# Two S5 half-units of the up-projection moved into the delta scan, and its first loads issued at the scan's start

## The chip, the cores and the metric

One core of a Trainium2 chip runs the whole kernel in one launch. The metric is the device time of that launch in microseconds (us), the median of the runs. TensorE (PE; its weight loads are PEld) multiplies into PSUM, which has 8 banks here (`P[:, 0..7, :]`); VectorE (DVE) and ScalarE (ACT) read PSUM; GpSimd (POOL) works on SBUF; SyncE (SP) issues most of the DMAs, in the order of its program, and waits on semaphores between them.

## The reference, cut to what matters

One step of a decoder block on 1024 prompt tokens and 8 x 4 sample tokens (NT = 1056 in all), D = 1024. A projection gives q, k, v, z, gates and the S5 input. Two branches run: a gated delta rule over chunks of 64 tokens, with 8 heads of 64, and an S5 branch. They are merged, and a mixture of experts follows:

```python
o = _rmsnorm(o, head_norm_w) * jax.nn.silu(z)          # o: output of the delta scan
y_a = o.reshape(bsz, t, DN_WIDTH) @ w_a_up             # 512 -> 1024
ys = ys * jax.nn.sigmoid(ys @ w_glu)                   # S5 branch
y_b = ys @ w_b_up                                      # 512 -> 1024
mixed = (sigmoid(gate_a) * y_a + sigmoid(gate_b) * y_b) @ w_o
x = x + mixed
x = x + _hier_moe(_rmsnorm(x, norm_ffn_w), ...)
```

All of it is float32. y_b needs only the S5 branch, which is done (and stored in DRAM as `y2_d`) before the scan begins.

## The kernel before, in words

The order of the work on each engine is written out by hand; engines meet through semaphores only. A large SBUF tile (`arena`) holds everything at hand-chosen offsets, so a load can only begin when what lay at its offset has been read.

**Delta scan** (L1041 to L1080 on PE, 16 chunks c = 0..15). PE in chunk c: state product (L1047, needs the state `s_S >= c+1`), query product (L1056), then for chunk c+1 the two products that need no state (`w_chunk` L1025, `u_chunk` L1036), then a wait for `s_kb` (POOL's scaled keys, L631) and `s_vn` (DVE's copy of the chunk's new values, L1739), then the state update product (L1066) and the output product (L1071). DVE in chunk c: copy `vn` (L1739), scale the state (L1740), add the update (L1742, sets `s_S`), then in the early chunks a step of the sample tokens' recurrence (L1695 to L1712), and in chunks 11 and 12 (`SQ_AT + 4`, `SQ_AT + 5`) two `head_norm`s each (L1730, L1732) for the first third of the tokens. PE's head sums for that third (L1079) are in chunks 8 and 9 and use banks 4 and 5; `s_rf` counts ACT's reads of them. Banks 0 and 1 take L1036/L1047, 2 and 3 the outputs, 6 and 7 the rest.

**Up-projection** (L1093 to L1107 on PE). The tokens are cut into three thirds of TBK = 352, the output features into KD = 8 blocks of 128: 24 units u, third u // 8, block u % 8. A unit is two halves of four matmuls (k = 0..3) of 128x128 by 128x352: the delta half `WAU` x `QT` and the S5 half `WBU` x `Y2`; a float32 matmul has two records in the trace. Units use the banks (0,1), (2,3), (4,5) in turn. After each of the first 8 units PE does a head sum (L1090) for the later thirds. DVE multiplies each half with its gate and adds (L1767 to L1769), and counts `s_yf`. Before u = 0 PE waits for `s_o2 >= 4` (head norms of the first third) and `s_wbu >= 32` (WBU and the first third of Y2 loaded); before every unit from 3 on for the read of the banks' last content.

**SP's queue** around it: at the scan's start (`s_S >= 1`) two loads of z (L2682) and the gate loads of units 0 to 3 (L2679); then, in chunks 9 to 12, the stores and the load for the sample tokens (L2693 to L2697); after `s_kb >= 48` (POOL has done its last chunk) the load of WBU (L2701, 2048 KB) and the three thirds of Y2 (L2703, 704 KB each), each third issued when the one before has landed; then the final state's store, the further gate loads (each behind `s_yf`) and W_O (L2717). Once the up-projection is done (`s_mix`), PE goes on with L1147 and SP with the loads of the next stage (L2720 and after).

Of the kernel before, what the change touches and what calls it, by code (L numbers as in the profile page):

```python
# [16 lines left out]
D = 1024  # L17
# [4 lines left out]
KD = D // 128  # L22
TT_ = (NT + 127) // 128
H, DH = 8, 64
HP = H // 2
C = 64
NC_ = SEQ // C
# [21 lines left out]
NBK = 3  # L49
TBK = NT // NBK  # L50
TSTRIP = NT // 4
KB0 = TBK // L
ARENA = 50020
# [18 lines left out]
def hybrid_step(nc, x_p, x_s, st_conv, st_delta, st_re, st_im, norm_mix, w_in, conv_w, a_log, dt_bias, head_norm,  # L72
# [4 lines left out]
    with ctx:  # L77
# [12 lines left out]
        y2_d = dram("y2_d", (SW // 128, 128, NT))  # L90
# [30 lines left out]
        def at(off, *dims):  # L121
            n = 1
            for d in dims:
                n *= d
            v = arena[:, off:off + n]
            if len(dims) == 2:
                return v.rearrange("p (a b) -> p a b", a=dims[0])
            if len(dims) == 3:
                return v.rearrange("p (a b c) -> p a b c", a=dims[0], b=dims[1])
            return v  # L130
# [5 lines left out]
        STG = WR + NWR * KD * 128  # L136
        stage = [at(STG + i * L * KS, L * KS) for i in range(2)]
        R = STG + 2 * L * KS
# [73 lines left out]
        QT = at(r, HP, NT)  # L212
# [5 lines left out]
        PRo = r + 4096  # L218
# [18 lines left out]
        WAU = at(WR, 4, D)  # L237
        MIX = at(R, KD, NT)
        PAIR = SEQ - 128
        PAIRED = NT - PAIR  # L240
        q = R + 8448 + HP * NT
        WBU = at(q, 4, D)
        x1 = at(q, TT_, D)
        GT = [at((5632, q + 9216)[j] + i * 2 * TBK, 2, TBK) for j in range(2) for i in range(4)]
        ZT = [at(q + 15360 + i * HP * TBK, HP, TBK) for i in range(2)]
        SQ2 = [at(o, HP, TBK) for o in (R + 4912, q + 18432, q + 18432 + HP * TBK)]
        OSN = at(ARENA - 1124, HP, 128)
        Y2 = at(q + 4096, 4, NT)
        SQ_AT = 7

        NWE = 3
# [72 lines left out]
        P = ctx.enter_context(nc.psum_tensor("P", [128, 8, 512], F32))  # L324
# [55 lines left out]
        s_selo = sem("s_selo")  # L380
# [13 lines left out]
        s_ou = sem("s_ou")  # L394
# [6 lines left out]
        s_rf = sem("s_rf")  # L401
# [4 lines left out]
        s_wbu = sem("s_wbu")  # L406
        s_gt = [sem("s_gt0"), sem("s_gt1")]
        s_ya = sem("s_ya")
        s_yf = sem("s_yf")
# [47 lines left out]
        s_inv = sem("s_inv")  # L457
# [240 lines left out]
        def _(pe):  # L698
# [51 lines left out]
            for i in range(TT_):  # L750
                n = rows(i)
                b = 6 - 2 * (i % 2)
                pe.wait_ge(s_xs, i + 1)
                pe.wait_ge(s_6f, max(i, 1))
                for k in range(KD):
                    m = pe.matmul(P[:, b + k // 4, 128 * (k % 4):128 * (k % 4) + n], xt[i][0:n, 128 * k:128 * k + 128],  # L756
                                  scale_of[i % 2][0:n, 0:n], start=True, stop=True)
# [59 lines left out]
            for a in range(GA):  # L817
                o = bank[:, 2 * GC * a:2 * GC * (a + 1)]
                pe.matmul(o, tmp[0][:, 128 * a:128 * a + 128], CTp[0][:, a].rearrange("p b c -> p (b c)"),
                          start=True, stop=False)  # L820
                m = pe.matmul(o, tmp[1][:, 128 * a:128 * a + 128], CTp[1][:, a].rearrange("p b c -> p (b c)"),
                              start=False, stop=True)
# [62 lines left out]
            for j in range(4):  # L885
                for q, (s0, sn) in enumerate(((0, 3), (3, 3), (6, 2))):
# [4 lines left out]
                    for k in range(4):  # L891
                        m = pe.matmul(bank[:, 0:sn * KS], wglu[:, k, 128 * j:128 * j + 128],  # L892
                                      ygT[:, k, s0:s0 + sn, :].rearrange("p a b -> p (a b)"),
                                      start=k == 0, stop=k == 3)
# [125 lines left out]
            def w_chunk(c):  # L1020
                pe.wait_ge(s_kb, 3 * c + 1)
                bank = bank7()
                for hp in range(HP):
                    for h in heads:
                        i = pe.matmul(bank[h, 64 * hp:64 * hp + 64], KB[c % 2][h, hp, :], TB[hp][h, c, :], start=True,  # L1025
                                      stop=True)
                i.then_inc(s_7, 1)

            def u_chunk(c):

                pe.wait_ge(s_kb, 3 * c + 2)
                if c >= 2:
                    pe.wait_ge(s_vn, c - 1)
                for hp in range(HP):
                    for h in heads:
                        pe.matmul(P[h, c % 2, 64 * hp:64 * hp + 64], TB[hp][h, c, :], VB[c % 2][h, hp, :],  # L1036
                                  start=hp == 0, stop=False, skip_group_check=True)

            w_chunk(0)
            u_chunk(0)  # L1040
            for c in range(NC_):  # L1041
                pe.wait_ge(s_wT, c + 1)
                pe.wait_ge(s_S, c + 1)
                S = S2[c % 2]
                for hp in range(HP):
                    for h in heads:
                        i = pe.matmul(P[h, c % 2, 64 * hp:64 * hp + 64], wT[c % 2][h, hp, :], S[h, hp, :],  # L1047
                                      start=False, stop=hp == HP - 1, skip_group_check=True)
                i.then_inc(s_vu, 1)

                if c >= 2:
                    pe.wait_ge(s_oc, c - 1)
                ob = P[:, 2 + c % 2, :]
                for hp in range(HP):
                    for h in heads:
                        pe.matmul(ob[h, 64 * hp:64 * hp + 64], S[h, hp, :], QT[h, hp, 64 * c:64 * c + 64], start=hp == 0,  # L1056
                                  stop=False, skip_group_check=True)
                if c + 1 < NC_:
                    w_chunk(c + 1)
                    u_chunk(c + 1)  # L1060
                pe.wait_ge(s_kb, 3 * c + 3)
                pe.wait_ge(s_vn, c + 1)
                bank = bank6()
                for hp in range(HP):
                    for h in heads:
                        i = pe.matmul(bank[h, 64 * hp:64 * hp + 64], KDr[c % 2][h, hp, :], vn[c % 2][h, hp, :],  # L1066
                                      start=True, stop=True)
                i.then_inc(s_6, 1)
                for hp in range(HP):
                    for h in heads:  # L1070
                        i = pe.matmul(ob[h, 64 * hp:64 * hp + 64], vn[c % 2][h, hp, :], KQ[h, hp, c, :], start=False,  # L1071
                                      stop=hp == HP - 1, skip_group_check=True)
                i.then_inc(s_ou, 1)
                if c in (SQ_AT + 1, SQ_AT + 2):
                    for hp in range(2 * (c - SQ_AT - 1), 2 * (c - SQ_AT)):
                        pe.wait_ge(s_sq2, hp + 1)
                        if hp >= 2:
                            pe.wait_ge(s_rf, hp - 1)
                        pe.matmul(P[:, 4 + hp % 2, 0:TBK], head_ones[:], SQ2[0][:, hp, :], start=True,  # L1079
                                  stop=True).then_inc(s_sm, 1)  # L1080
# [12 lines left out]
            for u in range(NBK * KD):  # L1093
                m, t = u % KD, TBK * (u // KD)
                if m == 0:
                    pe.wait_ge(s_o2, HP * (u // KD + 1))
                    pe.wait_ge(s_wbu, 16 * (2 + u // KD))
                if u >= 3:
                    pe.wait_ge(s_yf, u - 2)
                b = 2 * (u % 3)  # L1100
                for o, w, v in ((b, WAU, QT), (b + 1, WBU, Y2)):
                    for k in range(4):
                        i = pe.matmul(P[:, o, 0:TBK], w[:, k, 128 * m:128 * m + 128], v[:, k, t:t + TBK], start=k == 0,  # L1103
                                      stop=k == 3)
                i.then_inc(s_ya, 1)
                if u < 2 * HP:
                    head_sum(HP + u)  # L1107
# [218 lines left out]
        def _(dve):  # L1326
# [278 lines left out]
            for n in QSTEPS:  # L1605
                m = n - 1
# [150 lines left out]
            dve.sem_inc(s_os, 1)  # L1757
            dve.wait_ge(s_so, 1 + 64)
            for u in range(NBK * KD):
                b = 2 * (u % 3)  # L1760
                m, t = u % KD, TBK * (u // KD)
                dve.wait_ge(s_tb[u % 4], 32 + 16 * (u // 4 + 1))
                gt = GT[u if u < 4 else 4 + u % 4]
                ga, gb = gt[:, 0, :], gt[:, 1, :]
                ya, yb, o = P[:, b, 0:TBK], P[:, b + 1, 0:TBK], MIX[:, m, t:t + TBK]
                dve.wait_ge(s_ya, u + 1)
                link(dve.tensor_tensor(o, ya, ga, ALU.mult))  # L1767
                link(dve.tensor_tensor(gb, yb, gb, ALU.mult))
                dve.tensor_tensor(o, o, gb, ALU.add).then_inc(s_yf, 1)  # L1769
                dve.wait_ge(s_yf, u + 1)  # L1770
                if u in (4, 5, 9, 10):
                    j = {4: HP, 5: HP + 2, 9: 2 * HP, 10: 2 * HP + 2}[u]
                    head_norm(j)
                    head_norm(j + 1)
# [759 lines left out]
        def _(sp):  # L2534
# [140 lines left out]
            def gates(u):  # L2675
                m, t = u % KD, TBK * (u // KD)
                if u >= 4:
                    sp.wait_ge(s_yf, u - 3)
                sp.dma_start(GT[u if u < 4 else 4 + u % 4], gate_d[:, m, :, t:t + TBK].rearrange("j p t -> p j t")).then_inc(s_tb[u % 4], 16)  # L2679
# [4 lines left out]
            sp.wait_ge(s_S, 1)  # L2684
            gate_of_heads(0)
            gate_of_heads(1)
            for u in range(4):
                gates(u)

            sp.wait_ge(s_so, 1)  # L2690
            for v in range(2):
# [6 lines left out]
            sp.wait_ge(s_o2, HP)  # L2698
            gate_of_heads(2)
            sp.wait_ge(s_kb, 3 * NC_)  # L2700
            sp.dma_start(WBU, w_b_up[0].rearrange("(k p) n -> p k n", p=128)).then_inc(s_wbu, 16)  # L2701
            for t in range(NBK):
                sp.dma_start(Y2[:, :, TBK * t:TBK * t + TBK],  # L2703
                             y2_d[:, :, TBK * t:TBK * t + TBK].rearrange("k p t -> p k t")).then_inc(s_wbu, 16)
                sp.wait_ge(s_wbu, 16 * (2 + t))

            sp.wait_ge(s_S, NC_ + 1)
            for b in range(2):
# [105 lines left out]
```

## Time and profile before

| | us |
|---|---|
| median of 3 runs (lowest, highest) | 1516.19 (1514.94, 1517.57) |
| the profiled execution's own time | 1514.86 |
| its span, first to last instruction | 1513.1 |
| PE busy in the span | 1386.5 (92%) |
| DVE busy | 743.9 |
| DMA queue of SP and ACT (q1), share of 16 engines | 39.9% |

PE's idle time is spread in small pieces. The scan runs from about 770 to 845 us, the up-projection from 849.5 to 971 us. The granted clock (PEclk) is a share of full speed: 1.00 is 2.4 GHz and 0.50 is 1.2 GHz. In the names of transfers the numbers of buffers are left out, so `y_d` stands for `y2_d` at L2703. Busy spans of PE overlap a little (a matmul's end is modelled), so starts are the safer figures.

### The profile page before, as it was taken

How to read it: one execution, taken by the hardware profiler on the slowest of the kernel's cores; microseconds unless marked ns; L12 is line 12 of the kernel's file. 1: busy time of each engine (PE TensorE's matmuls, PEld its weight loads, DVE VectorE, ACT ScalarE, POOL GpSimd, SP SyncE). 2: the span in 40 equal slices, each digit the busy share in tenths (PEclk: the TensorE clock that was granted, in tenths of full speed). 3: DMA queues.
4: the chain of work that ended last, by engine and by line, in shares of the span. 5: the costliest groups of instructions: out<-in, count | busy, mean ns of one | idle time of the engine just before them, and what ended most of it. 6: DMA issues, size and time to landing. Idle time of an engine off the chain costs nothing.

```text
span 1513.1 us, 26998 instructions
## 1 busy us (share of the span) xinstructions
PE 1386.5 (92%) x11499; PEld 967.5 (64%) x11499; DVE 743.9 (49%) x1376; ACT 389.9 (26%) x707; POOL 147.5 (10%) x152
## 2 busy tenths in 40 slices
PE   7999999999999999999967899999978999999906
PEld 6667666666666656656767666765547888888802
DVE  4667695403425532689687344355553433222324
ACT  4211100114536553232213110011112333333312
POOL 1000010000001000045036000001111000000031
PEclk9998999999999999999989899999979999999958
DMA  5243684543522113233331425334348999999755
GB/s 170 82 102 57 188 239 134 134 122 103 140 62 62 44 44 99 53 99 119 92 136 32 157 69 187 108 131 155 112 154 326 420 425 426 426 425 425 304 183 195
DMA packets 190050, 262.54 MB, mean 174 GB/s; under 512 B 61219, under 2 KB 159889, under 8 KB 181465
## 3 DMA queue, kind: packets, MB, share of 16 engines
q1 hardware_dynamic: 164668, 200.39, 39.9%
q10 hardware_dynamic: 16988, 30.29, 5.4%
q0 software_dynamic: 8256, 29.89, 5.3%
q8 instruction: 103, 1.69, 0.5%
q14 instruction: 35, 0.28, 0.1%
HBM read 184.64 MB, written 75.90 MB: 172 GB/s over the span
## 4 chain that ended last, share of the span: by engine, by line
PE 75%; DVE 9%; DMA 5%; issue 5%; ACT 3%; POOL 2%; ACTq 0%; POOLq 0%; SPq 0%; DVEq 0%
PE P L730 28%; PE P L1103 8%; PE P L1292 6%; PE P L1190 5%; PE P L1261 4%; PE P L1289 3%; DMA arena<-in_w_expert_up_dram 2%; PE P L892 2%; POOL arena L631 2%; PE P L1226 1%; PE P L1265 1%; PE P L756 1%; PE P L1147 1%; DVE arena L1601 1%; PE P L954 1%
## 5 line engine op out<-in xcount | busy, mean ns | idle before, releaser
L730 PE MATMUL P<-arena 128*128 128x352 f32 x1680 | 520.8, 465 | 4.0 <-ACT arena L2363 2.8
L730 PEld LDWEIGHTS P<-arena 128*128 128x128 f32 x1680 | 315.9, 191 | 184.5 <-issue 23.4
L1289 PE MATMUL P<-arena 128*32 128x384 f32 x1536 | 172.8, 490 | 2.3 <-DMA arena<-in_w_expert_up_dram 2.3
L1292 PE MATMUL P<-arena 128*32 128x128 f32 x1536 | 174.9, 274 | 0.0
L1292 PEld LDWEIGHTS P<-arena 128*32 128x32 f32 x1536 | 165.8, 110 | 0.3
L1103 PE MATMUL P<-arena 128*128 128x352 f32 x384 | 117.9, 468 | 3.8 <-DMA arena<-y_d 3.8
L1103 PEld LDWEIGHTS P<-arena 128*128 128x128 f32 x384 | 74.4, 194 | 45.6 <-issue 6.1
L1261 PE MATMUL P<-arena 128*32 128x512 f32 (+1 forms) x768 | 89.5, 488 | 1.5 <-DVE arena L2013 1.5
L1265 PE MATMUL P<-arena 128*32 128x256 f32 x384 | 88.7, 380 | 0.0
L1190 PE MATMUL P<-arena 128*128 128x512 f32 x192 | 87.0, 598 | 0.0
L1965 DVE COPY arena<-P 128x512 f32<-128x512 f32 x24 | 16.6, 691 | 111.2 <-PE P L1226 109.9
L1289 PEld LDWEIGHTS P<-arena 128*32 128x32 f32 x1536 | 60.6, 110 | 6.5 <-DMA arena<-in_w_expert_up_dram 3.0
L2504 ACT ACTIVATE arena<-P 32x128 f32<-32x128 f32 x96 | 26.0, 270 | 141.9 <-PE P L1292 141.1
L2488 ACT ACTIVATE arena<-P 32x768 f32<-32x768 f32 (+2 forms) x56 | 45.0, 804 | 64.1 <-PE P L1265 63.9
L1976 DVE COPY arena<-P 32x256 f32<-32x256 f32 x96 | 40.4, 421 | 42.7 <-PE P L1265 41.6
L1190 PEld LDWEIGHTS P<-arena 128*128 128x128 f32 x192 | 34.9, 190 | 36.0 <-issue 35.9
L2091 ACT ACTIVATE arena<-P 128x1056 f32<-128x1056 f32 x20 | 21.0, 1050 | 134.9 <-PE P L730 134.2
L1620 DVE SCALAR_TENSOR_TENSOR arena<-arena,par 128x1024 f32<-128x1024 f32 x36 | 46.3, 1285 | 13.6 <-ACT arena L2296 12.7
L631 POOL TENSOR_TENSOR arena<-arena,N 128x256 f32<-128x256 f32 x48 | 44.7, 931 | 76.3 <-ACT arena L2387 26.0
L1767 DVE TENSOR_TENSOR arena<-P,arena 128x352 f32<-128x352 f32 x24 | 12.6, 525 | 77.7 <-PE P L1103 77.7
L1261 PEld LDWEIGHTS P<-arena 128*32 128x32 f32 x768 | 34.9, 109 | 19.4 <-issue 3.7
L1265 PEld LDWEIGHTS P<-arena 128*32 128x32 f32 x384 | 40.3, 110 | 10.5
(420 smaller groups left out, 1854.1 us busy)
## 6 DMA issues: line engine op xcount, KB each, us to landing
arena<-in_w_expert_up_dram SPq DMA_DIRECT2D x32, 2048.0 KB, 16.6
arena<-in_w_expert_down_dram SPq DMA_DIRECT2D x32, 1024.0 KB, 11.1
arena<-in_w_in_dram SPq DMA_DIRECT2D x36, 512.0 KB, 4.2
x_d<-zero SPq DMA_DIRECT2D x4, 3072.0 KB, 21.4
arena<-x_d POOLq DMA_DIRECT2D x24, 512.0 KB, 10.7
y_d<-arena ACTq DMA_DIRECT2D x24, 512.0 KB, 9.7
y_d<-zero SPq DMA_DIRECT2D x8, 1152.0 KB, 7.8
gate_d<-arena ACTq DMA_DIRECT2D x16, 528.0 KB, 4.3
```

The costliest lines, as they stand in the source:

```text
L631: pool.tensor_tensor(ring[c % 2], src[:, :, c, :], N1[:, q, :, c].unsqueeze(2).broadcast_to([128, HP, C]), ALU.mult).then_inc(s_kb, 1)
L730: m = pe.matmul(P[:, b + j, 0:TBK], w[:, k, :], hT[:, k, TBK * j:TBK * j + TBK], start=f, stop=l)
L892: m = pe.matmul(bank[:, 0:sn * KS], wglu[:, k, 128 * j:128 * j + 128], ygT[:, k, s0:s0 + sn, :].rearrange("p a b -> p (a b)"), start=k == ...
L1103: i = pe.matmul(P[:, o, 0:TBK], w[:, k, 128 * m:128 * m + 128], v[:, k, t:t + TBK], start=k == 0, stop=k == 3)
L1190: m = pe.matmul(P[:, b + o, :], MIX[:, k, 128 * i:128 * i + 128], W_O[:, k, 512 * o:512 * o + 512], start=k == 0, stop=k == KD - 1)
L1261: m = pe.matmul(P[strip_of(slot_of(i, s)[1]), b + o, 0:n], rows_of[s][:, k, :], WD[i % NWE][:, k, 512 * o:512 * o + n], start=k == 0, stop ...
L1265: m = pe.matmul(P[strip_of(slot_of(i, NSTRIP)[1]), b + o, FF * j:FF * j + FF], rows_of[s][:, k, :], WD[i % NWE][:, k, D - FF:D], start=k = ...
L1289: m = pe.matmul(P[strip_of(s), i % 2, 0:384], rows_of[s], WU[i % NWE][:, k, 128:512], start=k == 0, stop=k == KD - 1, skip_group_check=True)
L1292: m = pe.matmul(P[RT:128, i % 2, 128 * s:128 * s + 128], rows_of[s], WU[i % NWE][:, k, 0:128], start=k == 0 and s == 0, stop=k == KD - 1, ...
L1620: link(dve.scalar_tensor_tensor(acc[:, 0:SEQ], raw[:, i:i + SEQ], wcol, acc[:, 0:SEQ], ALU.mult, ALU.add))
L1976: m = dve.tensor_copy(yo[c % 3][strip_of(slot_), D - FF:D], P[last, 2 + 2 * (i % 2) + s // 2, FF * (s % 2):FF * (s % 2) + FF])
L2488: m = act.activation(yo[c % 3][h, 0:D - FF], wide[h, 0:D - FF], ACT.Copy)
```

## The change

The first three gate buffers, half of WBU at a time and the first third of Y2 get offsets that are free from the scan's start. SP loads them there; the S5 halves of units 0 and 1 are multiplied in chunks 11 and 12. `second_half` stands in PE's chunk after `u_chunk` and ahead of the waits for `s_kb` and `s_vn`. Unit 3's gate load and the second copy of WBU's upper half go to the end of the scan.

```diff
-        GT = [at((5632, q + 9216)[j] + i * 2 * TBK, 2, TBK) for j in range(2) for i in range(4)]
+        GT = [at(o, 2, TBK) for o in (R + 6400, R + 6400 + 2 * TBK, STG + 1024, q + 21248)]
+        GT += [at(q + 9216 + i * 2 * TBK, 2, TBK) for i in range(4)]
+        WBU_EARLY = [at(PRo, 2, D), at(5632, 2, D)]
+        Y2_EARLY = [at(o, TBK) for o in (7680, 7680 + TBK, STG + 1024 + 2 * TBK, ARENA - 612)]
+        def unit_banks(u):
+            return ((0, 5), (1, 4), (2, 3))[u] if u < 3 else (2 * (u % 3), 2 * (u % 3) + 1)
+        UNITS_READ = [0, 0, 0, 2, 3, 3]
+        def wbu(k, u):
+            return WBU[:, k, :] if k >= 2 and u >= KD else WBU_EARLY[k // 2][:, k % 2, :]
+        def y2(k, u):
+            return Y2_EARLY[k] if u < KD else Y2[:, k, TBK * (u // KD):TBK * (u // KD) + TBK]
...
+            def second_half(u):
+                for k in range(4):
+                    i = pe.matmul(P[:, unit_banks(u)[1], 0:TBK], wbu(k, u)[:, 128 * (u % KD):128 * (u % KD) + 128], y2(k, u),
+                                  start=k == 0, stop=k == 3)
+                return i
...
                     w_chunk(c + 1)
                     u_chunk(c + 1)
+                if c in (SQ_AT + 4, SQ_AT + 5):
+                    pe.wait_ge(s_wbu, 16 * 6)
+                    pe.wait_ge(s_rf, HP)
+                    second_half(c - SQ_AT - 4)
                 pe.wait_ge(s_kb, 3 * c + 3)
                 pe.wait_ge(s_vn, c + 1)
...
-                    pe.wait_ge(s_wbu, 16 * (2 + u // KD))
+                    pe.wait_ge(s_wbu, 16 * (6, 8, 9)[u // KD])
                 if u >= 3:
-                    pe.wait_ge(s_yf, u - 2)
-                (both halves of every unit)
+                    pe.wait_ge(s_yf, UNITS_READ[u] if u < len(UNITS_READ) else u - 2)
+                (the delta half; then)
+                if u >= 2:
+                    i = second_half(u)
...
             gate_of_heads(1)
-            for u in range(4):
+            sp.wait_ge(s_inv, 1)
+            sp.wait_ge(s_selo, HP)
+            for u in range(3):
                 gates(u)
+            for j in range(2):
+                sp.dma_start(WBU_EARLY[j], wb_view[:, 2 * j:2 * j + 2, :]).then_inc(s_wbu, 16)
+            for k in range(4):
+                sp.dma_start(Y2_EARLY[k], y2_d[k][:, 0:TBK]).then_inc(s_wbu, 16)
...
             sp.wait_ge(s_kb, 3 * NC_)
-            sp.dma_start(WBU, ...).then_inc(s_wbu, 16)
-            for t in range(NBK):
+            sp.dma_start(WBU[:, 2:4, :], wb_view[:, 2:4, :]).then_inc(s_wbu, 16)
+            for t in range(1, NBK):
                 sp.dma_start(Y2[:, :, TBK * t:TBK * t + TBK], ...).then_inc(s_wbu, 16)
-                sp.wait_ge(s_wbu, 16 * (2 + t))
+                sp.wait_ge(s_wbu, 16 * (7 + t))
+            sp.wait_ge(s_ou, NC_)
+            gates(3)
```

## Rows read from the trace of the kernel before

**Rows 1.** The page: busy us of each engine (share) xinstructions; shares of the chain that ended last.
```profile
PE 1386.5 (92%) x11499; PEld 967.5 (64%) x11499; DVE 743.9 (49%) x1376; ACT 389.9 (26%) x707; POOL 147.5 (10%) x152
PE 75%; DVE 9%; DMA 5%; issue 5%; ACT 3%; POOL 2%; ACTq 0%; POOLq 0%; SPq 0%; DVEq 0%
```
**Rows 2.** Chain of waits, 818 to 971 us: start, us, what.
```profile
818.36 1.38 PE P L1079 x4
...
838.89 10.49 DMA arena<-y_d
...
849.52 7.78 PE P L1103 x16
857.29 0.59 PE P L1090 x2
857.89 4.73 PE P L1103 x16
...
895.16 75.75 PE P L1103 x256
```
**Rows 3.** Timeline, chunks 11 and 12: start, us, engine, line [idle before <-releaser].
```profile
824.29 0.68 PE L1047 MATMUL P<-arena 64*64 64x64 f32 x16 [0.21 <-DVE arena L1742]
...
825.01 0.42 DVE L1739 COPY arena<-P 128x256 f32<-128x256 f32 x1 [0.87 <-PE P L1047]
...
826.12 0.58 PEld L1066 LDWEIGHTS P<-arena 64*64 64x64 f32 x16
...
827.52 0.68 PE L1047 MATMUL P<-arena 64*64 64x64 f32 x16 [0.21 <-DVE arena L1742]
...
828.88 0.58 PEld L1036 LDWEIGHTS P<-arena 64*64 64x64 f32 x16
...
830.77 0.42 DVE L1739 COPY arena<-P 128x256 f32<-128x256 f32 x1
...
831.26 0.68 PEld L1066 LDWEIGHTS P<-arena 64*64 64x64 f32 x16 [1.80 <-issue]
...
832.73 0.57 PEld L1047 LDWEIGHTS P<-arena 64*64 64x64 f32 x16 [0.33 <-issue]
```
**Rows 4.** Timeline, PE's last group before the up-projection.
```profile
845.32 0.40 PE L1085 MATMUL P<-shift_id,arena 32*128 32x32 f32 x4 [0.26 <-DVEq L1745]
```
**Rows 5.** Timeline, state products of chunks 1, 2, 3.
```profile
774.81 0.68 PE L1047 MATMUL P<-arena 64*64 64x64 f32 x16 [0.21 <-DVE arena L1742]
...
779.43 0.68 PE L1047 MATMUL P<-arena 64*64 64x64 f32 x16 [0.21 <-DVE arena L1742]
...
784.05 0.68 PE L1047 MATMUL P<-arena 64*64 64x64 f32 x16 [0.21 <-DVE arena L1742]
```
**Rows 6.** Windows of 2 us: busy by engine, then PEclk, DMA share, GB/s.
```profile
774.00:776.00 2.00, 1.79 (x62) 1.68 (x59) 1.61 (x2) 0.38 (x1) 1.18 (x2) 1.00 1.06 394
...
782.00:784.00 2.00, 1.15 (x32) 1.04 (x32) 1.31 (x4) 0.14 (x2) 1.33 (x3) 1.00 0.03 8
...
838.00:840.00 2.00, 2.00 (x43) 2.00 (x44) 0.76 (x2) 0.11 (x1) 0.45 (x1) 0.53 1.16 356
...
852.00:854.00 2.00, 2.00 (x5) 1.25 (x4) 0.00 (x0) 0.00 (x0) 0.00 (x0) 0.50 0.53 196
```
**Rows 7.** Timeline, state products of chunks 14 and 15, and the gap before 14.
```profile
836.54 0.68 PE L1066 MATMUL P<-arena 64*64 64x64 f32 x16 [1.69 <-issue]
...
837.89 0.97 PE L1047 MATMUL P<-arena 64*64 64x64 f32 x16 [0.21 <-DVE arena L1742]
...
842.67 0.68 PE L1047 MATMUL P<-arena 64*64 64x64 f32 x16 [0.21 <-DVE arena L1742]
```
**Rows 8.** Landing times of L2703 (Y2, x3), L2679 (gates, x24).
```profile
DMA to landing us min/median/max: 4.1/4.4/10.5
DMA to landing us min/median/max: 2.9/3.2/11.3
```
**Rows 9.** Timeline, the first of DVE's three operations on unit 0.
```profile
857.44 0.52 DVE L1767 TENSOR_TENSOR arena<-P,arena 128x352 f32<-128x352 f32 x1 [11.29 <-PE P L1103]
```

More of the change, by code:

```diff
@@ L1096, in _ @@
                     pe.wait_ge(s_o2, HP * (u // KD + 1))
-                    pe.wait_ge(s_wbu, 16 * (2 + u // KD))
+                    pe.wait_ge(s_wbu, 16 * (6, 8, 9)[u // KD])
                 if u >= 3:
-                    pe.wait_ge(s_yf, u - 2)
[L1100 to L1104, printed above, removed]
+                    pe.wait_ge(s_yf, UNITS_READ[u] if u < len(UNITS_READ) else u - 2)
+                for k in range(4):
+                    i = pe.matmul(P[:, unit_banks(u)[0], 0:TBK], WAU[:, k, 128 * m:128 * m + 128], QT[:, k, t:t + TBK], start=k == 0, stop=k == 3)
+                if u >= 2:
+                    i = second_half(u)
                 i.then_inc(s_ya, 1)
@@ L1759, in _ @@
             for u in range(NBK * KD):
-                b = 2 * (u % 3)
                 m, t = u % KD, TBK * (u // KD)
@@ L1764, in _ @@
                 ga, gb = gt[:, 0, :], gt[:, 1, :]
-                ya, yb, o = P[:, b, 0:TBK], P[:, b + 1, 0:TBK], MIX[:, m, t:t + TBK]
+                ya, yb, o = *[P[:, b, 0:TBK] for b in unit_banks(u)], MIX[:, m, t:t + TBK]
                 dve.wait_ge(s_ya, u + 1)
@@ L2686, in _ @@
             gate_of_heads(1)
-            for u in range(4):
+            sp.wait_ge(s_inv, 1)
+            sp.wait_ge(s_selo, HP)
+            for u in range(3):
                 gates(u)
+            wb_view = w_b_up[0].rearrange("(k p) n -> p k n", p=128)
+            for j in range(2):
+                sp.dma_start(WBU_EARLY[j], wb_view[:, 2 * j:2 * j + 2, :]).then_inc(s_wbu, 16)
+            for k in range(4):
+                sp.dma_start(Y2_EARLY[k], y2_d[k][:, 0:TBK]).then_inc(s_wbu, 16)
             sp.wait_ge(s_so, 1)
@@ L2700, in _ @@
             sp.wait_ge(s_kb, 3 * NC_)
-            sp.dma_start(WBU, w_b_up[0].rearrange("(k p) n -> p k n", p=128)).then_inc(s_wbu, 16)
-            for t in range(NBK):
+            sp.dma_start(WBU[:, 2:4, :], wb_view[:, 2:4, :]).then_inc(s_wbu, 16)
+            for t in range(1, NBK):
                 sp.dma_start(Y2[:, :, TBK * t:TBK * t + TBK],
                              y2_d[:, :, TBK * t:TBK * t + TBK].rearrange("k p t -> p k t")).then_inc(s_wbu, 16)
-                sp.wait_ge(s_wbu, 16 * (2 + t))
+                sp.wait_ge(s_wbu, 16 * (7 + t))
+            sp.wait_ge(s_ou, NC_)
+            gates(3)
             sp.wait_ge(s_S, NC_ + 1)
```

## The prediction

> **What bounds the kernel now.** The page first: PE is busy for 92% of the span, and 75% of the chain that ended last is PE [rows 1]. So a change pays only if PE's own work or PE's waits become less in the stage it touches, and everything behind it starts from PE. The chain of waits, read next over the stage, shows where PE is not the bound: at 838.89 it lies in the first Y2 load (queued behind WBU's, and issued when POOL had done its last chunk), stays there 10.49 us, and comes back to PE at 849.52 with unit 0 of the up-projection [rows 2]. The timeline says what PE did meanwhile: it finished the scan with the sample transposes at 845.32 + 0.40 = 845.72 and then stood still until 849.52, 3.8 us [rows 2, 4]. The same chain shows a second loss: unit 0 takes 7.78 us and every later unit 4.73 [rows 2]. The windows give the cause: the granted clock is 0.50 in 852 to 854 (1.2 GHz), after the standstill [rows 6]. From 895.16 on there is nothing but PE, 16 records per unit, without a wait, until 895.16 + 75.75 = 970.91 [rows 2]. The scan itself is bound by a ring PE, DVE, POOL whose gaps differ from chunk to chunk, so the question is which gap the moved work meets.
>
> **The change, part by part.** One matmul is two records of 4.73 / 16 = 0.296 us [rows 2], so the half of a unit is 8 records, 2.37 us.
>
> (a) Two S5 halves leave the up-projection: 2 x 2.37 = 4.73 us off PE, in a stage where PE is the bound. Nothing else is there to be late: DVE needs three operations of about 0.52 us per unit, 1.6 us, and even the shortened units 0 and 1 last 2.37 us and a head sum of 0.59 [rows 2, 9].
>
> (b) The standstill of 3.8 us [rows 2, 4] goes, since at the scan's end unit 0 waits for nothing that is still on its way. What is late next? Unit 0 needs only WAU, the head norms of the first third and early loads. The first head sum (L1090) needs ACT's squares of the next third, which in the trace follow the scan's end at once; unit 0's 2.37 us cover one of them. I take the whole 3.8; the least it can be is 3.5, if the start costs a wait as short as the 0.2 to 0.3 seen elsewhere [rows 3, 4].
>
> (c) Unit 0 ran at half clock after the standstill: 7.78 - 4.73 = 3.05 us [rows 2]. Without the standstill PE passes from the scan to dense matmuls at once, and I take all of it. Bounds: 0, if the clock is low there for another reason, and 3.05.
>
> (d) Chunk 11. `second_half(0)` stands in PE's order ahead of the state update. DVE's head norms of chunk 11 come after that update, so they cannot hide it. In the trace PE goes from L1036 straight to L1066 at 826.12 while its input, `vn`, has been there since 825.01 + 0.42 = 825.43 [rows 3]: no gap at all. So this half lies wholly on the path. Its price: four records of a head sum inserted in the same way took 1.38 us in the chain [rows 2], 0.20 more than 4 x 0.296; for 8 records 2.37 + 0.20 = 2.57 us. Queued behind it are the update, the output product and the next chunk of all three engines; they all move by 2.57. Bounds: 0, if something unseen covers it, and 4.7 + 0.2 = 4.9 at half clock.
>
> (e) Chunk 12. Now DVE's two head norms of chunk 11 (from about 827.52) delay `vn` of chunk 12 to 830.77, and PE, whose last weights of L1036 began at 828.88, could go on 0.47 us later (its step between such groups), at 829.35, but goes on at 831.26 [rows 3]: a gap of 1.91. It hides 1.91 of the 2.57; 0.66 us is left on the path. Bounds: 0 and 4.9 - 1.9 = 3.0. Chunk 13 has the like gap, behind the second pair of head norms (1.69 us [rows 7]), and gets nothing.
>
> (f) The early loads. Three gates of 352 KB, 2048 KB of WBU, 704 KB of Y2 and the two loads of z of 704 KB make 5.2 MB (before: four gates and the z, 2.8 MB); at 394 GB/s [rows 6] that is an estimated 13 to 14 us from about 771, landed by 785 to 790. PE wants them at 826: `s_wbu >= 96` and `s_rf >= 4` (ACT read the last head sum at about 820) cost nothing. Do they slow the chunks beside them? Chunk 1 to 2 with the DMA engines full took 779.43 - 774.81 = 4.62 us, chunk 2 to 3 with almost no DMA after 780 took 784.05 - 779.43 = 4.62 [rows 5, 6]. Nothing, so nothing is charged; the nearest bound on the other side is a few tenths.
>
> (g) The loads at the scan's end are shorter (half of WBU, two thirds of Y2), but unit 3's gates now stand behind both Y2 waits and `s_ou`. With the scan 3.2 us later, SP begins at about 841.7; WBU's half and Y2 no later than the 10.5 us of before, 852.2; the next Y2 4.4 (median) and the gates 3.2 [rows 8]: landed at about 860. DVE wants them with unit 3's product. Starting at 848.9, units 0 and 1 take 2.96 each, unit 2 5.32, unit 3's product is there at 864.9. Covered, by 5 us. Further gates, W_O, the second third's Y2 and upper half of WBU (needed at unit 8) have tens of us.
>
> (h) Chunk 14 ran at half clock: granted 0.53 in 838 to 840, and from state product to state product 842.67 - 837.89 = 4.78 us where chunk 11, with the same work at full clock, took 827.52 - 824.29 = 3.23 [rows 3, 6, 7]: 1.5 us lost. The gap of 1.69 us before it [rows 7] stays, so I let this loss stay too: 0, with bounds of -1.5 (it goes) and +1.5 (a second chunk falls as this one did).
>
> Sum: -4.73 - 3.8 - 3.05 + 2.57 + 0.66 = -8.35 us. The end of the up-projection moves from 971 to about 962.5. Behind it SP's loads for the next stage and PE's L1147 both start from its end, so the shift is passed on whole. Against the profiled execution's own time: 1514.86 - 8.4 = 1506.5. That execution was at the low end of the runs (1514.94 to 1517.57, median 1516.19); taken off the median, 1507.8, which I forecast.
>
> A rule that bears on (h): the Trainium skill, "TensorE: Matmul & The Clock Gate", Part 1, ties the fall of the clock to an idle engine and its return to activity. Read strictly, with the inserted work in chunks 11 and 12 the engine would be kept awake.
>
> **The rivals.**
>
> *The low stretch before chunk 14 goes too.* The two halves add 4.7 us of PE work within 10 us ahead of it. For it: more work of PE just ahead of the place. Against: the gap right before the fall is not filled [rows 7]. It would give 1.5 us more: 1507.8 - 1.5 = 1506.3. (This is the outcome that the page just named would have; the trace speaks half for it, since the clock fell with gaps of under 2 us, where the page thinks of an engine that stands idle.)
>
> *The half clock at the start of the up-projection stays.* A fall shortly before the scan's end would reach into unit 0. For it: chunk 14 fell, and a low stretch like it that begins one chunk later would lie partly in unit 0. Against: the low clock of unit 0 followed a standstill that is gone [rows 2, 6]. It costs up to 3.05: 1507.8 + 3.05 = 1510.8.
>
> *The gain is not passed on.* The path behind has stages with other limits (DMA in the chain is 5%, [rows 1]); if scatter and clock in them take back 4 to 8 us, the time is about 1514. Nothing in the rows speaks for it but that PE's clock is not the same in every execution.
>
> *Slower: unit 3's gates come too late.* Its place is DVE before unit 3; PE runs on until unit 6, which needs unit 3 read: 864.9 + 0.6 + 2 x 5.32 = 876.1. So the landing decides from 876.1 - 1.6 = 874.5 on, each us later costs one, and beyond 874.5 + 8.4 = 882.9 the kernel is slower than before; at 885 it would be 1516.2 + 2.1 = 1518.3. For it: three transfers in a row, each behind a wait, on one queue. Against: even with the longest landing of each row, 841.7 + 10.5 + 10.5 + 11.3 = 874.0 [rows 8].
>
> **How the numbers follow.** Forecast 1507.8: 0.62. Low stretch gone, 1506.3: 0.14. Half clock stays, 1510.8: 0.14. Not passed on, 1514: 0.08. Gates late, 1518.3: 0.02. The lower end: the forecast with -1.5 of (h), 0.66 of (e) hidden and about 1.3 of scatter (the runs' half width), 1504.4. The upper end: (c) lost and another chunk at half clock, 1507.8 + 3.05 + 1.5 = 1512.3. A change of under 0.2% (3.0 us) cannot be told from none; faster than 1513.2: the first three and a quarter of the fourth, 0.92; same: 0.05; slower, 0.03, of which 0.02 is the late gates and 0.01 things unseen.
>
> **What would show it.** (a) Units 0 and 1 with 8 records each. (b) The first matmul of unit 0 within 0.3 us of L1085. (c) Unit 2, the first whole one, at 4.73, and PEclk 1.00 from there. (d) L1066 of chunk 11 some 2.5 us later behind `vn` than before, and the state products of 11 and 12 5.8 us apart, not 3.23. (e) Those of 12 and 13 about 5.9 apart; before, 832.76 - 827.52 = 5.24 (832.73 is the start of chunk 13's weights) [rows 3]. (f) The chunks before 11 as before. (g) No idle of DVE before unit 3 on a DMA. Wrong would be: a wait on a DMA in chunk 11, a scan longer by more than 4 us, a low clock in the first units, or an up-projection that ends near 962 with a kernel that is not 8 us shorter.

## The result, and the profile after

| | before | changed |
|---|---|---|
| median as first measured (runs) | 1512.45 (6) | 1501.89 (6) |
| ratio, 95% interval | | 0.9927 [0.9898, 0.9956] |
| mean of the runs beside all kernels of this study | 1513.0 (98) | 1502.2 (19) |
| span of the profiled execution | 1513.1 | 1495.1 |

(The 18 further runs that repeat the kernel before, in the experiments, have a mean of 1513.3.)

The kernel became faster by 10.8 us (means), 0.7%, and the ratio's interval leaves out 1. Forecast were 8.4 us less and 1507.8 us, with a range from 1504.4: the time lies below the range. The forecast difference alone, 8.4 of 1512.45 us or a ratio of 0.9944, lies inside the interval; the parts below show what it was made of.

The page of the changed kernel, busy us and shares of the chain (before: [rows 1]):

```profile
PE 1379.1 (92%) x11499; PEld 963.3 (64%) x11499; DVE 742.3 (50%) x1376; ACT 390.2 (26%) x707; POOL 147.8 (10%) x152
PE 76%; DVE 8%; DMA 6%; issue 4%; ACT 3%; POOL 2%; ACTq 0%; POOLq 0%; SPq 0%; DVEq 0%
```

Its lines have moved: L1058 is `second_half`, L1070 the state product (L1047 before), L1093 the state update (L1066), L1128 the delta half of a unit (L1103), L1117 the head sum (L1090), L1173 the next stage (L1147), L1343 PE's first matmul of the last part (L1317). The chain of waits over the stage, start, us, what (before: [rows 2]):

```profile
822.49 2.56 PE P L1058 x8
825.05 0.64 PE P L1093 x16
...
828.44 2.56 PE P L1058 x8
831.00 0.61 PE P L1093 x16
...
844.80 0.40 PE P L1112 x4
845.20 2.56 PE P L1128 x8
847.77 0.59 PE P L1117 x2
848.36 2.37 PE P L1128 x8
...
853.68 2.37 PE P L1058 x8
...
960.89 17.65 PE P L1173 x128
```

The 10.49 us in a DMA are gone from the chain; PE passes from the transposes (844.80) to unit 0 (845.20) without a gap; unit 0's half takes 2.56 us and not twice that; units 0 and 1 have one half each. The window 846 to 852 says the same of the clock (its last columns: PEclk, DMA share, GB/s; before, 0.50 in [rows 6]):

```profile
846.00:852.00 6.00, 6.00 (x21) 3.82 (x21) 2.63 (x6) 3.36 (x8) 0.00 (x0) 1.00 0.46 135
```

The price, in the timeline of chunks 11 and 12 (before: [rows 3]):

```profile
820.41 0.68 PE L1070 MATMUL P<-arena 64*64 64x64 f32 x16 [0.21 <-DVE arena L1768]
...
821.13 0.42 DVE L1765 COPY arena<-P 128x256 f32<-128x256 f32 x1 [0.87 <-PE P L1070]
...
822.42 2.63 PE L1058 MATMUL P<-arena 128*128 128x352 f32 x8
...
826.36 0.68 PE L1070 MATMUL P<-arena 64*64 64x64 f32 x16 [0.23 <-DVE arena L1768]
...
829.60 0.42 DVE L1765 COPY arena<-P 128x256 f32<-128x256 f32 x1
...
832.30 0.68 PE L1070 MATMUL P<-arena 64*64 64x64 f32 x16 [0.22 <-DVE arena L1768]
```

In chunk 11 the copied values were there at 821.55 and PE worked on the half until about 824.98: 5.95 us from state product to state product, before 3.23. In chunk 12, 832.30 - 826.36 = 5.94, before 5.24.

Cut into three, the kernel shows what moved. "Stage" runs from the scan's first state product to the first matmul of the next stage; "middle" from there to the end of the last expert tile; "last part" from there to the last instruction. "Scan" is the part of the stage up to the end of PE's sample transposes:

| kernel (profiles) | scan | stage | middle | last part |
|---|---|---|---|---|
| before (3) | 75.5, 73.1, 73.8 | 202.6, 200.1, 201.4 | 468.9, 470.7, 468.0 | 71.5, 71.9, 73.0 |
| changed (3) | 78.6, 80.1, 79.6 | 194.3, 195.8, 195.3 | 468.1, 466.3, 471.1 | 66.1, 68.7, 66.9 |

In means the stage gives 6.3 us, the last part 4.9, and the middle is the same within its scatter of some 5 us. The last part is the surprise: nothing of the change is in it.

### The profile page after: what moved, and what is told of

The parts are those of the page before. It is cut to its first block, busy times and chain, and to the rows that moved or that the text cites. A ratio compares the mean times of both kernels' runs of the same rounds, so it can differ in the third digit from the quotient of the medians.

```text
span 1495.1 us, 27006 instructions
## 1 busy us (share of the span) xinstructions
PE 1379.1 (92%) x11499; PEld 963.3 (64%) x11499; DVE 742.3 (50%) x1376; ACT 390.2 (26%) x707; POOL 147.8 (10%) x152
## 4 chain that ended last, share of the span: by engine, by line
PE 76%; DVE 8%; DMA 6%; issue 4%; ACT 3%; POOL 2%; ACTq 0%; POOLq 0%; SPq 0%; DVEq 0%
PE P L747 28%; PE P L1318 6%; PE P L1216 5%; PE P L1058 4%; PE P L1128 4%; DMA arena<-in_w_expert_up_dram 4%; PE P L1287 3%; PE P L1315 3%; PE P L909 2%; PE P L1252 1%; PE P L1291 1%; PE P L1173 1%; DVE arena L1627 1%; PE P L879 1%; PE P L940 1%
## 5 line engine op out<-in xcount | busy, mean ns | idle before, releaser
L1318 PEld LDWEIGHTS P<-arena 128*32 128x32 f32 x1536 | 166.9, 111 | 0.6
L1315 PEld LDWEIGHTS P<-arena 128*32 128x32 f32 x1536 | 61.0, 111 | 6.5 <-DMA arena<-in_w_expert_up_dram 3.0
L1058 PE MATMUL P<-arena 128*128 128x352 f32 x192 | 60.9, 460 | 0.0
L1128 PE MATMUL P<-arena 128*128 128x352 f32 x192 | 60.8, 460 | 0.0
L1128 PEld LDWEIGHTS P<-arena 128*128 128x128 f32 x192 | 36.4, 190 | 20.1
L1058 PEld LDWEIGHTS P<-arena 128*128 128x128 f32 x192 | 36.3, 190 | 20.0
L1287 PEld LDWEIGHTS P<-arena 128*32 128x32 f32 x768 | 34.9, 109 | 19.4 <-issue 3.7
## 6 DMA issues: line engine op xcount, KB each, us to landing
arena<-x_d POOLq DMA_DIRECT2D x24, 512.0 KB, 10.8
```

Source lines behind the costliest of these rows:

```text
L1058: i = pe.matmul(P[:, unit_banks(u)[1], 0:TBK], wbu(k, u)[:, 128 * (u % KD):128 * (u % KD) + 128], y2(k, u), start=k == 0, stop=k == 3)
L1128: i = pe.matmul(P[:, unit_banks(u)[0], 0:TBK], WAU[:, k, 128 * m:128 * m + 128], QT[:, k, t:t + TBK], start=k == 0, stop=k == 3)
L1287: m = pe.matmul(P[strip_of(slot_of(i, s)[1]), b + o, 0:n], rows_of[s][:, k, :], WD[i % NWE][:, k, 512 * o:512 * o + n], start=k == 0, stop ...
L1315: m = pe.matmul(P[strip_of(s), i % 2, 0:384], rows_of[s], WU[i % NWE][:, k, 128:512], start=k == 0, stop=k == KD - 1, skip_group_check=True)
L1318: m = pe.matmul(P[RT:128, i % 2, 128 * s:128 * s + 128], rows_of[s], WU[i % NWE][:, k, 0:128], start=k == 0 and s == 0, stop=k == KD - 1, ...
```

## Experiments

**Both kernels again, unaltered.** For second and third profiles (the first of each is in the table above).

> The changed kernel once more, unaltered, timed beside the kernel before. Theory A (stage sum): it is 8.4 us shorter than before, in four parts that a second profile repeats: scan 3.2 us longer (770.2 to 845.7 us before: 75.5 us; here 78.7), standstill gone, unit 0 at full clock, two halves less; everything outside scan and up-projection differs only by what differs between two executions of one kernel. Theory B: the change also shortens what lies behind the up-projection (in the first profile 540.3 us before, 534.2 after), by another 5 to 6 us, and a second profile and the times show that again: 13 to 15 us shorter than before.

> The kernel before once more, unaltered, for a second profile. Theory A: scan 75.5 us with chunk 11 at 3.23 us, standstill 3.8 us, unit 0 at 7.8 us again; what lies before the scan and behind the up-projection differs from the first profile by several us (the changed kernel's profiles: 534.2 and 535.0 us behind it, two experiments 539.0 and 543.8), which shows that this part is scatter and not the change. Theory B: behind the up-projection it takes 540 us again, within 1 us.

> The kernel before, third profile. Behind the up-projection its first two took 540.3 and 542.5 us, five kernels with the changed scan 533.9 to 543.8. If that part is scatter alone, this one may lie anywhere in 534 to 544; if the change shortens it by 4 to 6 us (theory B), it lies at 540 or above again. From the scan's first state product to the next stage: 200.1 to 202.6 us again.

> The changed kernel, third profile. Scan's first state product to next stage 194.3 to 195.7 us again, or 1.5 less if chunk 14 runs at full clock (then 192.8 to 194.2). Behind it 534.2 and 535.0 us so far: scatter alone allows 534 to 544, theory B wants below 536. Time 8 to 9 us below before.

Measured: the changed kernel 1503.14 (ratio 0.9941 [0.9919, 0.9963]) and 1502.15 (0.9923 [0.9906, 0.9941]); the kernel before against itself 1.001 [0.9991, 1.0029] and 1.0 [0.9987, 1.0012]. Chunk 11 is 3.23, 3.23, 3.23 before and 5.95, 5.95, 5.95 after. What lies behind the up-projection as a whole (middle and last part) is 540.3, 542.5, 541.0 us before and 534.2, 535.0, 538.0 after: the two sets don't overlap, but 538.0 is above the 536 that theory B wanted, and theory B says nothing of where. The whole times decide nothing either: the medians are 9.3 and 11.8 us below before, where theory A wanted 8.4 and theory B 13 to 15. Nor did the scan repeat as expected. Chunk 14 ran at full clock in the second and third profile of before and in the third of the changed kernel, and there the stage was 195.3 us, not the expected 192.8 to 194.2. The time was lost in chunk 15, which took 4.47 us and not 3.06. Its state product stops after 14 of its 16 records, at full clock and with no wait in the profile:

```profile
847.32 0.27 PE L1070 MATMUL P<-arena 64*64 64x64 f32 x1 [1.12 <-issue]
```

In the second profile of before, the chain of waits at the scan's end:

```profile
836.35 10.07 DMA arena<-y_d
846.42 0.14 issue
846.55 6.65 PE P L1103 x16
```

The standstill is 4.9 us there and not 3.8, since the scan ended at 841.63 (chunk 14 at full clock: 3.22 us, not 4.78) while the load, begun at POOL's last chunk, landed no sooner after it; and unit 0 took 6.65 us, not 7.78. So the standstill and unit 0's slow start trade against each other. From the scan's end to the next stage the kernel before takes 127.1, 127.1 and 127.6 us in its three profiles (standstills of 3.8, 4.9 and 5.0 us, unit 0 at 7.78, 6.65 and 7.12 us), and the changed kernel 115.7 in all three.

**Loads only: the halves go back to units 0 and 1.**

```diff
-                if c in (SQ_AT + 4, SQ_AT + 5):
-                    ...
-                    second_half(c - SQ_AT - 4)
-                if u >= 2:
-                    i = second_half(u)
+                i = second_half(u)
```

> The early loads stay, the two S5 halves go back from chunks 11 and 12 into units 0 and 1. Theory A: scan as long as before (75.5 us), up-projection without standstill and at full clock, 4.7 us longer than in the changed kernel; in all 6.9 us shorter than before, and 4.73 - 3.23 = 1.5 us longer than the changed kernel. Rival: halves put in chunks are hidden, so this is 4.7 us longer than the changed kernel.

Measured: 1507.25 us, 0.9965 [0.9949, 0.9981]. Chunk 11 is 3.23 us again, and from the scan's end to the next stage it takes 120.4 us against 115.7 in the changed kernel: 4.7 more, two halves. Against the 2.7 + 0.7 us that the halves cost in chunks 11 and 12, moving them is worth 1.3 us. Stage 194.1 us, with chunk 14 at full clock (1.5 us of luck). The early loads alone bring most of the stage's gain. The whole is 5.3 us below before by the ratio, expected were 6.9. The whole time is 4 us above the changed kernel, as the rival wanted, but its last part is 71.2 us (below), so it is no proof of the rival.

The early loads have a price that this kernel shows by itself, since it has them without the halves. In chunk 3, after 351 matmul records counted from the scan's first, PE stops inside a group with no wait in the profile:

```profile
784.37 0.27 PE L1053 MATMUL P<-arena 64*64 64x64 f32 x1 [1.31 <-issue]
```

All fifteen profiles of kernels with the early loads have this pause at this very record (0.76 to 1.59 us), and none of the five without them (before, and before with redundant waits, below). Chunk 3 takes 4.8 us in place of 4.4, in means; chunks 0 to 10 together take 54.3 in place of 53.4.

**Halves in chunks 12 and 13.**

```diff
-                if c in (SQ_AT + 4, SQ_AT + 5):
+                if c in (SQ_AT + 5, SQ_AT + 6):
                     ...
-                    second_half(c - SQ_AT - 4)
+                    second_half(c - SQ_AT - 5)
```

> The two halves in chunks 12 and 13, behind the head norms, in place of 11 and 12. Theory A: chunk 11 is 3.23 us again from state product to state product; each half meets a gap of 1.91 and 1.69 us and leaves 0.7 and 0.9 us on the path; 1.7 us shorter than the changed kernel, 10 us shorter than before. Rival: the gap moves away from the work (DVE's copy comes later as well), so nothing is won: same as the changed kernel within 0.3 us.

> Halves in chunks 12 and 13 once more, for a comparison of whole times: by the stages (191.9 us from the scan's first state product to the next stage, of which 1.5 is chunk 14 at full clock by luck) it is 1.9 us shorter than the changed kernel; the whole times may not be able to tell that.

Measured: 1500.4 (0.992 [0.9899, 0.994]) and 1500.91 (0.9923 [0.9907, 0.994]); mean of 12 runs 1500.1. Chunk 13 in the timeline:

```profile
835.23 0.68 PE L1070 MATMUL P<-arena 64*64 64x64 f32 x16 [0.22 <-DVE arena L1768]
...
837.24 2.63 PE L1058 MATMUL P<-arena 128*128 128x352 f32 x8
839.80 0.68 PE L1093 MATMUL P<-arena 64*64 64x64 f32 x16
...
841.17 0.68 PE L1070 MATMUL P<-arena 64*64 64x64 f32 x16 [0.22 <-DVE arena L1768]
```

5.94 us, before 5.13; chunk 12 5.94, before 5.24; chunk 11 3.23. The halves cost 0.7 + 0.8 us where the changed kernel pays 2.7 + 0.7. Stage 192.0 and 190.5 us, both with chunk 14 at full clock, so that some 1.5 us of the distance to the changed kernel are not the placing. The gap stays where it was.

**The eight matmuls spread over chunks 10, 12 and 13.**

```diff
+                if c == SQ_AT + 3:
+                    ... waits as before ...
+                    second_half(0, (0, 1))
+                if c == SQ_AT + 5:
+                    second_half(0, (2, 3))
+                    second_half(1, (0,))
+                if c == SQ_AT + 6:
+                    second_half(1, (1, 2, 3))
```

> The eight matmuls spread over the gaps: two in chunk 10 (gap 1.2 us), three in chunk 12 (1.9), three in chunk 13 (1.7). Theory A: what each leaves on the path is 0.2, 0.1 and 0.3 us, so the scan is about 0.5 us longer than before, and the kernel 2.7 us shorter than the changed one, 11 us shorter than before. Rival: every insertion costs the drain and restart of the matmul pipeline, 0.5 us or more each, and it is no better than halves in chunks 12 and 13.

> The spread matmuls once more: by the stages (191.3 us) 0.7 us shorter than halves in chunks 12 and 13 and 2.6 us shorter than the changed kernel. Its first whole times (ratio 0.9943) did not show that, with 543.8 us behind the up-projection; if that was scatter, the ratio now comes out at 0.991 to 0.993.

Measured: chunks 10, 12, 13 at 4.76, 5.65, 5.35 us (before 4.62, 5.24, 5.13), 0.8 us in all; stage 191.3 and 191.2 us. But the whole is 1502.72 (0.9943 [0.9922, 0.9965]) and 1503.2 (0.9939 [0.9917, 0.9961]), no better than the changed kernel, and the last part is 72.3 and 72.6 us in both profiles. The expectation of 0.991 to 0.993 fell, and with it the thought that the last part is mere scatter.

**One half more in chunk 11.** `second_half(0)` is done twice there.

> The half of unit 0 is multiplied twice in chunk 11 (its price doubled). Theory A: chunk 11 has no gap, so it goes from 5.95 to 8.3 us from state product to state product, one half more being 2.37 us; chunk 12 stays at 5.94. Rival: a part of the price was the switch between kinds of matmul or the wait instructions, then less than 2.2 us are added.

The timeline (a single run, 1504.79 us):

```profile
824.43 0.68 PE L1070 MATMUL P<-arena 64*64 64x64 f32 x16 [0.21 <-DVE arena L1770]
...
826.44 5.00 PE L1058 MATMUL P<-arena 128*128 128x352 f32 x16
...
832.75 0.68 PE L1070 MATMUL P<-arena 64*64 64x64 f32 x16 [0.23 <-DVE arena L1770]
```

8.32 us: 2.37 more. In chunk 11 every matmul is paid in full, and some 0.35 us come on top once (2.72 - 2.37).

**The standstill put back, bare and filled.** In both, unit 0 waits for the last third of Y2; in the second PE does unit 0's delta half twice, for nothing, while it waits.

```diff
-                    pe.wait_ge(s_wbu, 16 * (6, 8, 9)[u // KD])
+                    (second kernel only: 2 x 4 matmuls WAU x QT into P[:, 0, :] if u == 0)
+                    pe.wait_ge(s_wbu, 16 * (9, 9, 9)[u // KD])
```

> The changed kernel, but unit 0 waits for the last third of Y2, so that PE stands still at the scan's end as it did before. In the changed kernel's first profile those loads land about 5 us after the scan. Theory A: standstill about 5 us, then some 10 records at half clock, which costs about 3 us more: the up-projection ends 8 us later than in the changed kernel, counted from the scan's end. Rival: the half clock of unit 0 has nothing to do with the standstill: only 5 us later.

> As the run with the standstill, but PE fills the wait with 16 records of the delta half of unit 0, done twice for nothing into the bank that unit 0 then overwrites (4.7 us). Theory A: no record at half clock in unit 0, and the up-projection ends about 5 us later than in the changed kernel, 3 us earlier than with the bare standstill, though PE has more work. Rival: the clock is low there whatever PE does: as late as with the standstill, 8 us.

The chains of waits, bare and then filled:

```profile
850.27 4.20 DMA arena<-y_d
854.48 0.14 issue
854.61 5.03 PE P L1128 x8
859.64 0.75 PE P L1117 x2
860.40 2.37 PE P L1128 x8
```
```profile
845.09 4.13 DMA arena<-y_d
849.22 0.04 issue
849.27 2.63 PE P L1132 x8
851.90 0.59 PE P L1117 x2
```

Bare: a standstill of 854.61 - 850.23 = 4.4 us, and unit 0's half takes 5.03 us, the granted clock being 0.50 (window 855 to 859). Filled: the same load keeps unit 0 waiting even longer, 849.27 - 844.04 = 5.2 us, but unit 0's half takes 2.63 us at 1.00 (window 849.3 to 853). From the scan's end to the next stage the changed kernel takes 115.7 us, the bare one 122.7, the filled one 121.0: 7.0 and 5.3 more, where theory A wanted 8 and 5 and the rivals 5 and 8. The half clock came from the standstill; work that is thrown away keeps it off. (One profile each. A low clock in chunk 14 is not the cause: the second and third profile of before had none and a slow unit 0 all the same, and the first two of the changed kernel had it and a fast unit 0.) Whole times 1508.77 (0.9975 [0.9956, 0.9995]) and 1508.46 (0.9967 [0.9948, 0.9986]) can't tell the two apart.

**What the last part hangs on.** It begins with PE's jump over the expert tiles that aren't needed. In the chain of the kernel before it is:

```profile
1441.65 33.86 issue
1475.51 1.22 PE P L1317
1476.73 1.81 issue
1478.55 2.07 PE P L1317 x2
```

and in the changed kernel:

```profile
1429.00 33.47 issue
1462.47 3.41 PE P L1343 x4
```

A second pause stands between PE's first matmuls in all three profiles of before (1.81, 2.07, 1.79 us) and in loads-only (2.02), and in none of the changed kernel. The two pauses together are 37.1 us before and the one of the changed kernel 33.4, in means: 3.7 of the 4.9 us. The spread kernel has no second pause, but its first is longer (38.70 and 39.14 us).

The engines' waits name nothing here, but the DMA view does. Between the first and second matmul of before (window 1475.51 to 1478.55) exactly one packet moves, on queue q8, of the kind that the page calls instruction, 16 KB:

```profile
DMA packets 1, 0.02 MB, mean 5 GB/s; under 512 B 0, under 2 KB 0, under 8 KB 0
q8 instruction: 1, 0.02, 2.1%
```

It ends at 1477.13, and PE goes on 1.4 us later. In the other two profiles of before and in loads-only PE goes on 1.3 to 1.5 us after such a packet, too. In the spread kernel the like packet ends before PE's first matmul (at 1468.75, PE starts at 1470.20); in the changed kernel it ends at 1464.46, when PE has begun its third, and no pause follows. The pauses in chunks 3 and 15 end in the same way, 1.2 to 1.5 us after an instruction packet. So PE seems to wait there for its own program. That fits every profile, but it is read from them and was not tested by itself.

Four kernels only add redundant waits on a semaphore that was reached long before, and so move PE's later program:

```diff
             pe.wait_ge(s_wau, 16)
+            for _ in range(4):          # or 16
+                pe.wait_ge(s_wau, 16)
             for u in range(NBK * KD):
```

> The kernel before with 4 redundant waits on PE ahead of unit 0, where PE stands still anyway. Theory C (place of PE's program): the last part, 72.1 us before (mean of three), changes by several us, to about 67 or 69, or the pause of 2 us behind PE's first matmul goes; scan and up-projection as before. Rival (the change's data and transfers): 71.5 to 73 again, with the second pause.

> The kernel before with 16 redundant waits on PE at the same place. Theory C: the last part is another than 72.1 us in at least one of the two padded kernels, by over 2 us. Rival: 71.5 to 73.

> The changed kernel with 4 redundant waits on PE ahead of unit 0 (0.2 us on the path). Theory C: the last part, 67.2 us in the changed kernel (mean of three), can rise to 70 to 73. Rival: 66 to 69 as in the changed kernel.

> The changed kernel with 16 redundant waits on PE at the same place (0.8 us on the path). Theory C: the last part is over 70 us in at least one of the two padded kernels, as in the kernel with spread matmuls. Rival: 66 to 69.

The kernel before with 4 waits, same place in its chain:

```profile
1438.20 32.38 issue
1470.58 3.78 PE P L1319 x4
```

| kernel | last part, us | median, us | ratio to before |
|---|---|---|---|
| before + 4 | 67.4 | 1507.94 | 0.9973 [0.9953, 0.9994] |
| before + 16 | 67.4 | 1508.86 | 0.9979 [0.9966, 0.9992] |
| changed + 4 | 67.6 | 1501.28 | 0.9933 [0.9897, 0.9968] |
| changed + 16 | 67.9 | 1504.03 | 0.9942 [0.9924, 0.996] |

Four instructions that do nothing make the kernel before 4.7 us shorter in its last part (67.4 us with 4 and with 16 waits, one profile each) and faster as a whole. That the padded changed kernel would get worse, as theory C wanted for one of the two, did not happen. So theory C stands for the kernel before, and the data and transfers of the change are not needed for a short last part: its length went with how many PE instructions lie ahead of it. That the changed kernel's last part is short for the same reason is the simplest reading; no run shows it by itself.

**Both findings together.** The spread kernel with the same redundant waits:

> Matmuls spread over chunks 10, 12 and 13, with 4 redundant waits on PE ahead of unit 0. If the last part hangs on the place of PE's program: 67 to 68 us there in place of 72.5, the scan's first state product to the next stage 191.3 us, the whole 1498 us against 1502 for the changed kernel and 1513 for before. Rival: the spread matmuls cause the 72.5, and it stays: 1503.

> The same with 16 redundant waits (0.8 us on the path): 1499 us, or 1503 if its last part stays at 72.5 while that with 4 waits goes down (then the place matters in steps between 4 and 16).

Measured: 1497.91 us, 0.9897 [0.9878, 0.9917], and 1498.44, 0.9898 [0.9881, 0.9915]. The chain's jump with 4 waits:

```profile
1430.81 34.69 issue
1465.50 2.93 PE P L1350 x3
```

Last part 68.1 and 67.3 us (spread without waits 72.3 and 72.6), stage 189.8 and 190.2. So the spread matmuls were not the cause of their long last part. The version with 4 waits beats both kernels, by 14.4 us and by 3.6 in the means of its 6 runs (1498.6).

## Why the prediction was right and wrong

(a) Two halves off the up-projection: 4.73 forecast, 4.7 measured between loads-only and the changed kernel.

(b, c) Right, shown by the standstill put back and filled. The split 3.8 + 3.05 holds only for the first profile; the second has 4.9 + 1.9 (6.65 - 4.73), the third 5.0 + 2.4. Here I read one execution's split as the kernel's, but the sum is 6.8, 6.8 and 7.4. With (a), the forecast for the stretch from the scan's end to the next stage was 4.73 + 3.8 + 3.05 = 11.6 us less, and 11.6 is what the means of three show. The Trainium skill, "TensorE: Matmul & The Clock Gate", Part 1, says that the same kernel has a different number of slow matmuls at its start from run to run; behind the standstill here the traces show the like (7.78, 6.65 and 7.12 us for the same unit).

(d) 2.57 forecast, 2.72 measured three times. That the first half meets no gap was right. The price was read from a head sum's own piece of the chain; the half's own piece is 0.19 us above its matmuls as forecast (2.56), but the update behind it takes 0.64 in place of 0.48, and that was not in it.

(e) 0.66 forecast, 0.70 measured.

(f) No wait in chunk 11, but "nothing is charged" for the early loads was wrong. The prediction compared two chunks of the kernel before, whose loads are over ahead of chunk 3. Chunks 0 to 10 take 53.3 to 54.1 us before and 53.8 to 55.2 after, 0.9 more in means. The pause in chunk 3, which the loads-only kernel has without the halves, gives some 0.4 of it; the rest may be scatter.

(g) Unit 3's gates did not hold DVE.

(h) The loss stays, but not in every execution: chunk 14 takes 4.78, 3.22, 3.22 us before and 4.71, 4.77, 3.22 in the changed kernel. Over all twenty profiles it is slow in 2 of 5 of the kernels with before's scan, in 5 of 8 with work added in chunk 11, and in none of the 7 others; so few cannot say whether the place of the halves has a part in it. The standstill did not hide the loss: from chunk 14's start to the next stage the kernel before takes 134.9 us with it and 133.3 and 134.0 without, since a shorter standstill was followed by a slower unit 0; the changed kernel takes 123.5 with it, the one with halves in chunks 12 and 13 takes 122.0 without. In the means of three it adds 0.5 us, and the pause in chunk 15 another 0.4.

Sum over the stage: 8.35 forecast, 8.3 between the first two profiles (202.6 - 194.3), 6.3 between the means of three. That the first two agree with the forecast is luck: both have the slow chunk 14, and their chunks 0 to 10 are alike. The 2.1 us that the means lack are all in the scan: 0.9 in chunks 0 to 10, 0.2 in (d) and (e), 0.5 in chunk 14 and 0.4 in chunk 15.

The prediction failed at its last step, "behind it ... the shift is passed on whole", and at the reference. The last part became 4.9 us shorter on top, and four redundant waits give the kernel before the same; the prediction had no such term, and its only rival for that region took gain away. And the range was taken around 1516.19 with 1.3 us of scatter, the half width of three runs: the next three runs of the same kernel took 1508.2 to 1510.0, and 98 runs have a mean of 1513.0 and reach from 1507.3 to 1517.9. With 1513.0 the same sum gives 1504.6, still 2.4 above the 1502.2 measured. So of the 5.6 us between 1507.8 and 1502.2 the reference gave 3.2 and the last part 4.9; the stage took back 2.1, and the rest, 0.4, is within the scatter of the middle. That the two errors of the sum partly cancel is luck.

## What to carry to other kernels

Work put into a gap must stand, in its engine's program order, behind the event that makes the gap: the head norms of chunk 11 open the gap of chunk 12, and the half in chunk 11 was paid in full. Read the gap per chunk and cut the work to it. Ask what each part brings: here the early loads gave most, and the two halves, placed as they were, only 1.3 us. When a kernel gains or loses a few us where nothing was edited, take more profiles and compare the parts before giving the gain to the edit: 4.0 us of the 10.8 here (means 1513.0 and 1509.0) were to be had with four waits that do nothing.

## What the runs showed of the hardware

- The pause of PE at the jump to the kernel's last part is 32.4 to 39.1 us long, and in some programs a second one of about 2 us follows PE's first matmul. Both repeat from execution to execution of one program, the first within 2.1 us (33.86, 35.73, 35.91 before), and change with a few instructions ahead of them. No wait in the profile names their cause. The second pause ends 1.3 to 1.5 us after a packet of 16 KB of instructions in all four profiles that have it.
- The same kind of pause comes inside groups of matmuls. With the early loads running PE stops for 0.76 to 1.59 us after 351 records of the scan in fifteen profiles of fifteen, without them in none of five; in chunk 15 it stops for 1.12 us in one profile of the changed kernel. PE goes on 1.2 to 1.5 us after an instruction packet each time.
- Putting 128x352 matmuls between groups of 64x64 ones in chunk 11 costs 0.35 us once beyond the matmuls (2.72 us for one half, 2.37 for a second behind it).
